# Two loads of token rows moved ahead of a store, and the order of the final loads of the sums changed, in a decoder layer's kernel

## The reference, cut to what matters

```python
x = layer_norm(ALPHA * x + fox_mixer(x, ...), ln1_g, ln1_b)
scores = sigmoid(x @ w_router)                     # 8 of 64 experts per token
routed = sum over chosen e of w[e] * ((silu(x @ w_gate[e]) * (x @ w_up[e])) @ w_down[e])
shared = (silu(x @ ws_gate) * (x @ ws_up)) @ ws_down
out = layer_norm(ALPHA * x + routed + shared, ln2_g, ln2_b)
```

## Time and profile before

| what | value |
|---|---|
| runs of before | 1783.9, 1787.21, 1788.5 us |
| median | 1787.21 us |
| the profiled execution's own time | 1784.81 us |
| span of its trace | 1783.1 us |
| busy in the span | PE 1607.1 us (90%), DVE 1186.9 (67%), ACT 1026.2 (58%), POOL 472.7 (27%) |
| mean granted TensorE clock | 0.958 of 2.4 GHz |
| chain that ended last | PE 57%, issue 12%, DVE 11%, DMA 8%, ACT 7%, POOL 2% |

### The profile page before, as it was taken

One profiled execution on the slowest core, in us unless ns is written; L12 is line 12 of the kernel. 1 busy time (PEld: TensorE's weight loads), 2 busy tenths in 40 slices (PEclk: granted clock), 3 DMA queues, 4 the chain that ended last, 5 costly groups with the idle time before them and its releaser, 6 DMA issues.

```text
span 1783.1 us, 31788 instructions
## 1 busy us (share of the span) xinstructions
PE 1607.1 (90%) x8238; PEld 1312.7 (74%) x8239; DVE 1186.9 (67%) x2022; ACT 1026.2 (58%) x1688; POOL 472.7 (27%) x486
## 2 busy tenths in 40 slices
PE   7999999999997899799999999999899999999960
PEld 5897777778776687578777778777777777787740
DVE  3214777777676576745677777767776777778736
ACT  3115666666665443426666776666666667677733
POOL 0000000000000125341444444443344434444420
PEclk9999999999998898899999999999999999999985
DMA  4423222222223333656999999988998999999956
GB/s 167 132 77 92 66 54 59 65 51 61 58 48 125 135 108 107 216 173 228 315 282 286 304 361 323 298 271 250 315 293 250 285 334 302 363 335 335 369 129 261
DMA packets 161508, 369.26 MB, mean 207 GB/s; under 512 B 53040, under 2 KB 73520, under 8 KB 161456
## 3 DMA queue, kind: packets, MB, share of 16 engines
q1 hardware_dynamic: 136272, 284.21, 46.6%
q0 software_dynamic: 25184, 84.39, 18.8%
HBM read 294.39 MB, written 65.77 MB: 202 GB/s over the span
## 4 chain that ended last, share of the span: by engine, by line
PE 57%; issue 12%; DVE 11%; DMA 8%; ACT 7%; POOL 2%; DVEq 1%; another core or an unknown queue 1%; POOLq 1%; ACTq 0%; SPq 0%
PE bank L962 5%; PE bank L968 5%; PE bank L965 5%; PE out_ps L1020 3%; DMA x_rows<-rows_scratch,gidx 3%; DMA sums_scratch<-ys,sidx 3%; PE out_ps L1021 3%; PE q_ps L952 3%; PE out_ps L870 3%; PE k_ps L997 3%; ACT probs L1186 3%; PE k_ps L989 2%; PE k_ps L990 2%; DVE nm L1536 2%; PE k_ps L849 2%
## 5 line engine op out<-in xcount | busy, mean ns | idle before, releaser
L1759 DVE TENSOR_TENSOR gu_lo<-raw_gu,gu_hi 128x1024 fp32r<-128x1024 f32 x260 | 306.8, 1222 | 20.2 <-ACT gu_hi L1286 18.9
L1286 ACT CAST gu_hi<-raw_gu 128x1024 fp32r<-128x1024 f32 x260 | 252.7, 1048 | 0.0
L962 PE MATMUL bank<-gu_hi,xb_hi 128*128 128x512 f32 x576 | 236.0, 410 | 2.0 <-ACT ex L1276 1.3
L965 PE MATMUL bank<-gu_lo,xb_hi 128*128 128x512 f32 x576 | 228.4, 397 | 0.0
L1759 DVE TENSOR_TENSOR dn_lo<-raw_dn,dn_hi 128x1024 fp32r<-128x1024 f32 x130 | 154.5, 1209 | 0.5 <-ACT dn_hi L1286 0.5
L1197 ACT CAST pt_hi<-k_ps 128x512 fp32r<-128x512 f32 (+1 forms) x192 | 85.8, 481 | 118.8 <-PE k_ps L849 118.4
L642 POOL DMA_INDIRECT sums_scratch<-ys,sidx x64 | 113.5, 1774 | 127.4 <-DMA sums_scratch<-ys,sidx 73.4
L968 PE MATMUL bank<-gu_hi,xb_lo 128*128 128x512 f32 x576 | 146.2, 395 | 0.0
L1286 ACT CAST dn_hi<-raw_dn 128x1024 fp32r<-128x1024 f32 x130 | 129.5, 1047 | 0.0
L962 PEld LDWEIGHTS bank<-gu_hi,xb_hi 128*128 128x128 f32 x576 | 110.1, 191 | 26.3 <-issue 2.7
L968 PEld LDWEIGHTS bank<-gu_hi,xb_lo 128*128 128x128 f32 x576 | 108.0, 187 | 26.4
(11 more groups left out here) (267 smaller groups left out, 4008.3 us busy)
## 6 DMA issues: line engine op xcount, KB each, us to landing
raw_gu<-in_moe_w_gate_dram SPq DMA_DIRECT2D x128, 512.0 KB
raw_gu<-in_moe_w_up_dram SPq DMA_DIRECT2D x128, 512.0 KB
raw_dn<-in_moe_w_down_dram SPq DMA_DIRECT2D x128, 512.0 KB
wqk<-in_fox_w_in_dram SPq DMA_DIRECT2D x66, 128.0 KB, 2.5
v_scratch<-v_out SPq DMA_DIRECT2D x32, 256.0 KB, 2.8
va<-v_scratch SPq DMA_DIRECT2D x16, 512.0 KB, 4.7
xs<-in_x_dram SPq DMA_DIRECT2D x8, 512.0 KB, 7.4
wv<-in_fox_w_in_dram SPq DMA_DIRECT2D x4, 1024.0 KB, 7.5
```

The costliest lines, as they stand in the source:

```text
L962: i = pe.matmul(o3, xb_hi[s][:, c], g_hi[:, :, c], start=c == 0, stop=False, skip_group_check=True)
L965: pe.matmul(o3, xb_hi[s][:, c], g_lo[:, :, c], start=False, stop=False, skip_group_check=True)
L1286: a.copy(hi, raw).then_inc(S[done], 1)
L1759: dve.tensor_tensor(lo, raw, hi, ALU.subtract).then_inc(S[lo_ok], 1)
```

## The change

In SP's queue the loads of the rows of tiles 2 and 3 go ahead: tile 2's ahead of `tile(7)`, behind `turned` 1; tile 3's between `tile(7)` and `weights_out(6)`, behind `turned` 2. Tiles 4 to 7 stay in the loop. At the end, g2 and b2 are loaded once TensorE has done the last gate and up product; only one tile of `sums_scratch1` is loaded before the last addition has landed, and the other seven follow one by one between the tiles of `sums_scratch0`. No computation changes, and the number of DMAs is the same.

```diff
--- before.py
+++ after.py
@@ -497,13 +497,18 @@
             load_down(0, ws_down, free)
             load_gate_up(1, w_gate[0], w_up[0], free)
             load_down(1, w_down[0], free)
+            sp.wait_ge(S["x1_stored"], 16 * (TT - 1))
+            sp.wait_ge(S["turned"], 1)
+            load_rows(2)
             tile(TT - 1)
+            sp.wait_ge(S["turned"], 2)
+            load_rows(3)
             weights_out(TT - 2)
             sp.wait_ge(S["x1_stored"], 16 * TT)
             for b in range(2, SH):
-
-                sp.wait_ge(S["turned"], b - 1)
-                load_rows(b)
+                if b > 3:
+                    sp.wait_ge(S["turned"], b - 1)
+                    load_rows(b)
                 if b == 4:
                     weights_out(TT - 1)
                 elif b == 5:
@@ -527,19 +532,19 @@
 
             def load_sums(j, t):
                 sp.dma_start((fin0[:, t], fin1(t))[j], sums[j][t * P:(t + 1) * P, :]).then_inc(tile_in[t], 16)
+            sp.wait_ge(S["gated"], SH + E)
+            sp.dma_start(g2[:], ln2_g.to_broadcast([P, D])).then_inc(S["c_loads"], 16)
+            sp.dma_start(b2[:], ln2_b.to_broadcast([P, D])).then_inc(S["c_loads"], 16)
             sp.wait_ge(S["g_lo_ok"], G_PIECES * (E + 1))
             sp.wait_ge(S["set_free"], 1)
             sp.wait_ge(S["summed"], 1)
-            for t in range(TT):
-                load_sums(1, t)
+            load_sums(1, 0)
             for i in range(2):
                 sp.wait_ge(sent[i], 8 * E + SENT_0[i])
-            load_sums(0, 0)
-            sp.dma_start(g2[:], ln2_g.to_broadcast([P, D])).then_inc(S["c_loads"], 16)
-            load_sums(0, 1)
-            sp.dma_start(b2[:], ln2_b.to_broadcast([P, D])).then_inc(S["c_loads"], 16)
-            for t in range(2, TT):
+            for t in range(TT):
                 load_sums(0, t)
+                if t + 1 < TT:
+                    load_sums(1, t + 1)
             for t in range(TT):
                 sp.wait_ge(S["f_out"], t + 1)
                 sp.dma_start(out[t * P:(t + 1) * P, :], fin2[:, t]).then_inc(stored, 16)
```

## The result

| | runs | median | lowest to highest |
|---|---|---|---|
| before | 8 | 1787.93 us | 1783.9 to 1790.52 |
| after | 8 | 1778.6 us | 1770.3 to 1782.93 |

The ratio after to before is 0.9939, with a 95% interval of 0.9922 to 0.9957. It is faster by 0.61%, or 10.9 us of 1787.9; the plain difference of the medians is 9.3 us. Forecast were 1772.7 us and a range of 1768 to 1779: the direction is right, the median stands 0.4 us inside the upper end, and about a quarter of the forecast gain of 14.5 us is missing by the ratio, a third by the medians. The profiled execution of after took 1778.78 us, with a span of 1777.1 us.

What follows compares the result with a forecast made beforehand. Bound by TensorE in the experts, but by late rows in the shared expert and by DMAs and VectorE in the last norm. Gains 5.0 + 9.5 = 14.5 us take 1787.2 to 1772.7 us; range 1768 to 1779.

Steps and rivals of the forecast that it cites:

- First edit: Shared expert: rows of tiles 2 and 3 loaded earlier, so the first down product ends at 758.1, not 763.1; 5.0 us.
- 2.95 is nearest the first, so I take full clock: TensorE's new 2.95 us wait before the down product: clock stays up, as after 2.88 us; 5.0 us gained, otherwise 3.2.
- The first rival: Shared expert: down product restarts at half clock after the new wait; gain 3.2 + 9.5 = 12.7, 1774.5 us; chance 0.20.
- Paid back before 787: Shared expert: GpSimd's lists or the routing keep their time, TensorE only waits later; gain 9.5, 1777.7 us; chance 0.12.
- The nameless wait: ScalarE's unexplained 2.5 us wait near 772, forecast to stay; as a rival it goes too: 17.0 gained, 1770.2 us; chance 0.07.
- Second edit: Last norm: g2 and b2 early, one tile of sums before the landing; first reciprocal at 1742.7, not 1752.24; 9.5 us.
- plus 0.3 for part of that load: Last addition with one load in front: 6.0 us alone plus 0.3, landing at 1734.6 instead of 1738.5.
- the shortest load of a burst, 3.7: Last norm: first tile of sums takes 3.7 us from issue to landing, so it is there at 1738.3.
- The addition lands as late as now: End: the late start comes from GpSimd's side, not SP's loads; gain 5.0 + 5.6 = 10.6, 1776.6 us; chance 0.12.
- The rule of turns: DMA queues alternate packet by packet; by it the addition's late start has another cause and the end gains 5.6 us.
- The slower rival: Expert loop runs at another phase between gathers and weight loads; up to 13 us slower, 1800 us; chance 0.03.
- The sum: Shared expert and last norm together: 5.0 + 9.5 = 14.5 us, 1787.2 - 14.5 = 1772.7 us.

Runs made afterwards that it cites:

- e_beside0: Changed kernel with no tile of sums loaded beside the last addition, its first load waiting for the landing too; 1769.23 us in a single execution.
- e_filler: Changed kernel with 24 idle transposes in TensorE's wait for the low part of the down weights; copies 1 to 11 took 101.70 us against 103.16.
- e_rows: Kernel before with only the loads of the rows of tiles 2 and 3 moved ahead; 1789.04 us against 1791.69, ratio 0.9988.
- e_end: Kernel before with only the end changed (g2 and b2 early, one tile of sums before the landing); 1786.4 us, ratio 0.9965.
- e_vectors: Kernel before with only g2 and b2 loaded early, all eight loads of sums still ahead of the last landing; ratio 0.9990.
- e_down_first: Changed kernel with VectorE making the low parts of the shared down weights and x1's last tile before tile 6's routing; 1777.67 us, ratio 0.9921.

## Why the prediction was right or wrong

**The reading of what bounds the kernel** held. Both waits that were named (rows behind the store and the token weights; the sums behind eight loads) were the ones that went, and the stage behind 781 kept what had been gained.

**First edit: the mechanism was right, the size came out 3.3 us and not 5.0.** By distance from the first copy, `dn_lo` was forecast at 21.7 us (755.3 - 733.6) and was there at 21.8 (750.29 and 2.35, less 730.89). The product started 3.0 us earlier than before (21.90 us behind the first copy against 24.92) and ended 3.1 us earlier, where full clock was to give 5.0. The step that failed is "2.95 is nearest the first, so I take full clock": the wait came out at 3.27 us, the product's first eight matmuls took 3.44 us against 3.52 before, and the clock was at its lower level. The wait is 0.3 us longer since the transposes came 0.16 us sooner behind the first copy than forecast and the product started 0.15 us behind `dn_lo`; by the prediction's own choice of the nearest row, 3.27 would have pointed at the 3.41 and half clock. Two rows, 2.88 and 3.41 us, with the wait between them, were too little to choose by, and the length of the wait is not all that counts: in e_beside0 the clock fell 2.2 us into it. The first rival (3.2 us) was the right size; it had 0.20. e_filler shows that the clock made 1.5 us of the missing 1.7; the product's length at full clock, 3.0 us and not 2.8, accounts for the rest.

**Paid back before 787:** it wasn't. The gain at the fifth copy is 3.3 us as well (53.82 to 50.54), and e_rows keeps it alone.

**The nameless wait** was to stay, and it stays in part. In after the wait of 2.5 us is gone from tile 3's copy, and one of 3.9 us stands before tile 2's, where TensorE does not need the copy yet; the routing's own wait, 3.41 us before 778.80, is 3.25 us now. The waits of after:

```profile
ACT xb_hi L1312 <- remote: 3.9, 1, 3.9
ACT ys L1328 <- remote: 3.3, 1, 3.3
DVE pos L1709 <- remote: 2.1, 1, 2.1
```

On chip B e_rows has it at tile 2's copy and e_end at tile 3's, as after and before on chip A, but e_vectors and e_down_first at neither. No trace of chips C and D has such a wait there, the unchanged kernel's included, where TensorE's wait for the routing is 0.57 us. So whether it comes goes with the chip or the session more than with the edit. What it is stays open.

**Second edit: 7.3 us and not 9.5**, with the mechanism right. The landing was forecast 3.9 us earlier and came 2.3 earlier: 7.94 us, not 6.3. The term "plus 0.3 for part of that load" was mis-sized; one load beside it cost 0.9 to 2.4 us over the 6.08 of none. From the landing to VectorE's first addition it took 4.4 us (12.35 - 7.94), not 3.8; the shortest load of a burst, 3.7, was taken for the first load behind a landing, which measured 3.8 to 4.3 wherever one load stood ahead. The rest, 1.8 us because the reciprocal now hangs on ScalarE's root and not on b2, came out as worked out (4.33 us after the start against 4.29). No tile of sums was late later: the rest is 30.90 us against 30.86. The vectors cost nothing that a run can show.

**The addition lands as late as now:** refuted by the series from none to eight loads. The rule of turns in the Trainium skill (DMA: Bandwidth & Descriptors, "Queues, rings and completion order"), which would have given this outcome, does not describe the late start: with four or eight loads the addition's packets began only five us after its issue, against 2.1 alone, while SP's loads moved. Once they have begun the two share (0.52 MB beside 0.97 from 1733.5 to 1738.6 before), as the rule has it. The stages' gain of 10.6 us is the figure that this rival had (5.0 + 5.6), by coincidence: neither of its two terms came out.

**The slower rival** (another phase of the loop) is not seen in any run. What it named is real in size: the loop differs by 14 us between two executions of one kernel. It strikes both kernels alike.

**The sum.** 3.3 + 7.3 = 10.6 against 14.5: of the 3.9 us missing, 1.7 belong to the clock and 2.2 to the landing and the first load. Of the 1.7, e_filler shows 1.5. From 1787.2 this gives 1776.6; the median was 1778.6, the rest being within the scatter of either. That the median fell inside the range is in part luck: its high end was drawn for a first edit that is paid back, and what filled the room instead were two terms that were each too large, a case that the rivals priced one at a time and never together.

## What to carry to other kernels

When a load is moved out of a wait, look up what the waiting engine needs next and when that is ready; here it was a low part of weights 3 us later, and making that first gave another 3.4 to 5.1 us. Do not put loads in a queue beside the last transfer that everything waits for: those it has to wait for anyway go before it, the others behind. And judge a change of half a per cent by the stages it touches, not by the spans of two profiled executions.

## What was not expected of the hardware

- One load of 512 KB beside an accumulating transfer of 512 KB made it land 0.9 to 2.4 us later, four 4.2 us later, eight no more than four. Its first packet moved 2.1 us after its issue alone, and 5.0 to 5.4 us with four or eight. These are not equal turns from the start. Whether they are an order of arrival, no run settles: only four of the eight loads had been issued when the addition's first packet would be due, and 1.0 to 1.2 MB, two loads' worth, had moved when it came. The mechanism stays open.
- TensorE's clock fell to its lower level in or right behind a wait of 3.23 to 3.27 us in all five traces that have it, 2.2 to 3.1 us after TensorE fell idle in four and 0.6 us after the restart in e_rows; it stayed up in e_down_first (1.23 us) and in e_filler (0.57 us), and across 2.88 us.
- A stretch in which both the engines and the DMAs are near full (0.97) ran from 884.0 to 898.5 us in thirteen executions, of which the edits touch at most the last 25 us. Where its microseconds come from was not tried.
- The same kernel needed 110.73 us for copies 1 to 11 on one chip and 106.18 on another; TensorE's wait for the routing is 2.8 us shorter there (3.41 against 0.57). The rest is open.
